# The feed-forward block's up projection takes x times the norm's weights; the norm's root multiplies the projections in their banks

## The reference, cut to what matters

```python
def rms_norm_2(x, g):
    xf = x.astype(jnp.float32)
    y = xf * lax.rsqrt(jnp.mean(xf * xf, axis=-1, keepdims=True) + EPS)
    return (y * g.astype(jnp.float32)).astype(x.dtype)

def conv_ffn_2(h, w_up, conv_w, conv_b, w_down):
    a = h @ w_up
    a = lax.conv_general_dilated(a, conv_w[:, None, :], ...) + conv_b   # 3 taps along the tokens, each channel by itself
    g, u = jnp.split(a, 2, axis=-1)
    return (jax.nn.gelu(g, approximate=True) * u) @ w_down

for l in range(DEPTH_2):
    ...
    x = x + rms_norm_2(memory_cross_attention(h, mem_n, ...), mem_post_g[l])
    h = rms_norm_2(x, ffn_pre_g[l])
    x = x + rms_norm_2(conv_ffn_2(h, ffn_w_up[l], ffn_conv_w[l], ffn_conv_b[l], ffn_w_down[l]), ffn_post_g[l])
```

## Time and profile before

| | |
|---|---|
| device time, median of 3 runs | 3171.85 us (3171.47 to 3172.96) |
| device time of the profiled execution | 3170.39 us |
| its span in the trace | 3168.6 us |
| busy of the span: PE, DVE, ACT, POOL | 2932.6 us (93%), 1545.3 (49%), 1279.6 (40%), 329.7 (10%) |
| mean clock granted to PE | 0.962 of full speed |

### The profile page before, as it was taken

One profiled execution on the slowest core, in us unless ns is written; L12 is line 12 of the kernel. 1 busy time (PEld: TensorE's weight loads), 2 busy tenths in 40 slices (PEclk: granted clock), 3 DMA queues, 4 the chain that ended last, 5 costly groups with the idle time before them and its releaser, 6 DMA issues. The chain is left out here.

```text
span 3168.6 us, 38772 instructions
## 1 busy us (share of the span) xinstructions
PE 2932.6 (93%) x14576; PEld 2294.1 (72%) x14576; DVE 1545.3 (49%) x2161; ACT 1279.6 (40%) x1866; POOL 329.7 (10%) x286
## 2 busy tenths in 40 slices
PE   6989887999989999899899889999899999899997
PEld 2879765688768888576577668886675677578885
DVE  3357246565545443356663454443465663454433
ACT  3751424532243332534563343333425652433333
POOL 0010004500001100004000111100004001011100
PEclk8999999999999999999799999999999899999999
DMA  5100210045412222120032122222120131122222
GB/s 234 67 28 1 87 53 1 7 167 169 149 68 105 93 93 93 62 80 14 27 120 80 53 80 93 93 104 78 68 80 1 45 129 54 53 93 94 105 102 80
DMA packets 43552, 254.04 MB, mean 80 GB/s; under 512 B 4608, under 2 KB 6784, under 8 KB 15872
## 3 DMA queue, kind: packets, MB, share of 16 engines
q1 hardware_dynamic: 43392, 251.87, 22.3%
HBM read 249.75 MB, written 2.10 MB: 79 GB/s over the span
## 5 line engine op out<-in xcount | busy, mean ns | idle before, releaser
L238 DVE TENSOR_TENSOR ring_lo<-ring,ring_hi 128x2048 fp32r<-128x2048 f32 x201 | 460.8, 2293 | 807.5 <-ACT ring_hi L231 807.5
L231 ACT ACTIVATE ring_hi<-ring 128x2048 fp32r<-128x2048 f32 x201 | 383.8, 1909 | 456.0 <-PE bank L289 341.0
L289 PE MATMUL bank<-h_hi,ring_hi 128*128 128x512 f32 x1360 | 546.5, 402 | 17.1 <-DVE mix_lo L1605 6.4
L289 PE MATMUL bank<-h_hi,ring_lo 128*128 128x512 f32 x1360 | 534.3, 393 | 0.0
L1417 PE MATMUL bank<-h_hi,ring_hi 128*128 128x512 f32 x960 | 374.2, 390 | 5.7 <-DVE ring_lo L238 5.7
L1421 PE MATMUL bank<-h_hi,ring_lo 128*128 128x512 f32 x960 | 373.5, 389 | 0.0
L1420 PE MATMUL bank<-h_lo,ring_hi 128*128 128x512 f32 x960 | 373.5, 389 | 0.0
L289 PEld LDWEIGHTS bank<-h_hi,ring_hi 128*128 128x128 f32 x1360 | 257.2, 189 | 80.9 <-issue 15.6
L289 PEld LDWEIGHTS bank<-h_hi,ring_lo 128*128 128x128 f32 x1360 | 257.1, 189 | 60.0
L289 PE MATMUL bank<-h_lo,ring_hi 128*128 128x512 f32 x624 | 243.9, 391 | 0.0
L1417 PEld LDWEIGHTS bank<-h_hi,ring_hi 128*128 128x128 f32 x960 | 180.2, 188 | 45.4 <-issue 5.5
(11 more groups left out here) (453 smaller groups left out, 5018.2 us busy)
## 6 DMA issues: line engine op xcount, KB each, us to landing
ring<-in_stream SPq DMA_DIRECT2D x209, 1024.0 KB, 4.8
mod_w<-in_stream SPq DMA_DIRECT2D x64, 256.0 KB, 5.1
xT<-in_xT SPq DMA_DIRECT2D x2, 2048.0 KB, 14.8
const<-in_const SPq DMA_DIRECT2D x1, 2306.5 KB, 15.8
par<-in_par SPq DMA_DIRECT2D x3, 696.0 KB, 4.0
memT<-in_memT SPq DMA_DIRECT2D x2, 1024.0 KB, 4.8
out<-xT SPq DMA_DIRECT2D x1, 2048.0 KB, 6.3
ctxT<-in_ctxT SPq DMA_DIRECT2D x1, 1024.0 KB, 4.8
```

Source lines behind the costliest of these rows:

```text
L231: nc.scalar.activation(self.slab_hi(slab + j), self.slab(slab + j), ACT.Copy).then_inc(slab_rounded, 1)
L238: nc.vector.tensor_tensor(lower, self.slab(slab + j), self.slab_hi(slab + j).bitcast(F32), ALU.subtract)\
L289: ins = nc.tensor.matmul(out, lhsT, rhs, start=start and w is w_hi and x is x_hi, stop=stop and w is w_lo)
```

## The change

The next norm's squares, their sums and the second root leave `project`, and with them the scaling of `xT` into `hT`. The stage ends behind the first root. A new class `Unnormed` takes the place of `Norms` in the second block's `ffn`: DVE scales the projected tiles and adds them to `xT`, ACT writes `h_hi` from `xT` times the gain, DVE writes `h_lo` with the gain in the same instruction, ACT squares `xT`, and DVE adds up the squares. PE sums them over the channels in one matmul behind the first two pairs, and then ACT takes the root. In `taps` DVE multiplies both banks of each pair by the root; only then may ACT's `centers` read them. In `project`, ACT also copies banks 1 to 3 into `raw`, so that PE may write these banks early.

```diff
+        class Unnormed:
+            def banks_left(self, pe):
+                pe.wait_ge(self.post.scale_ready.sem, self.post.scale_ready.at(1))
+                pe.wait_ge(self.post.left.sem, self.post.left.at(len(self.post.LEFT)))
+            def sum(self, pe):
+                pe.wait_ge(self.squares_added.sem, self.squares_added.at(KT - 1))
+                nc.tensor.matmul(bank[:, 6, :], con("ones"), self.square_place(0), start=True, stop=True).then_inc(self.summed.sem, 1)
+            def scalar(self, act):
...
+                    nc.scalar.activation(split_hi(n), xT[:, n, :], ACT.Identity, scale=self.gain(n)).then_inc(self.upper_ready.sem, 1)
+                    if n == 1:
+                        self.halfway_scalar(act)
+                    if n >= SQUARES:
+                        act.wait_ge(self.squares_added.sem, self.squares_added.at(n - SQUARES + 1))
+                    nc.scalar.activation(self.square_place(n), xT[:, n, :], ACT.Square).then_inc(self.squared.sem, 1)
+                act.wait_ge(self.summed.sem, self.summed.at(1))
+                root_of_mean(act, self.scale, bank[:, 6, :]).then_inc(self.scale_ready.sem, 1)
+            def vector(self, dve):
+                post, LAG = self.post, 2
+                dve.wait_ge(post.scale_ready.sem, post.scale_ready.at(1))
+                dve.wait_ge(post.left.sem, post.left.at(len(post.LEFT)))
+                for n in range(KT + LAG):
+                    if n < KT:
+                        src = post.raw[:, n, :] if n == 0 or n in post.LEFT else bank[:, n, :]
+                        nc.vector.scalar_tensor_tensor(post.raw[:, n, :], src, post.gain(n), post.scale, ALU.mult, ALU.mult)\
+                            .then_inc(post.normed.sem, 1)
+                        if n not in post.pool_tiles:
+                            dve.wait_ge(post.normed.sem, post.normed.at(n + 1))
+                            nc.vector.tensor_tensor(xT[:, n, :], xT[:, n, :], post.raw[:, n, :], ALU.add)\
+                                .then_inc(post.added_by_dve.sem, 1)
+                    if n >= LAG:
+                        k = n - LAG
+                        dve.wait_ge(self.upper_ready.sem, self.upper_ready.at(k + 1))
+                        nc.vector.scalar_tensor_tensor(split_lo(k), xT[:, k, :], self.gain(k), split_hi(k).bitcast(F32),
+                                                       ALU.mult, ALU.subtract).then_inc(self.lower_ready.sem, 1)
+                    if n == 3:
+                        self.halfway_vector(dve)
+                    if n >= 5:
+                        self.add_square(dve, n - 4)
+                for n in range(KT + LAG - 4, KT):
+                    self.add_square(dve, n)
...
@@ ffn, tensor: two_pairs and what follows
+                        for k in range(AHEAD):
+                            for n in range(2):
+                                first = part_of(n, k)
...
+                        for k in range(AHEAD):
+                            for n in range(2, 4):
+                                part_of(n, k)
...
                 two_pairs()
+                if norm.late:
+                    norm.sum(pe)
@@ ffn, scalar
                 def centers(n, j):
-                    act.wait_ge(pair_done.sem, pair_done.at(n + 1))
+                    done = norm.scaled if norm.late else pair_done
+                    act.wait_ge(done.sem, done.at(n + 1))
@@ ffn, vector
                 def taps(n, j):
+                    out_ap = pair(j)
+                    if norm.late:
+                        dve.wait_ge(pair_done.sem, pair_done.at(n + 1))
+                        for s in range(2):
+                            last = nc.vector.tensor_tensor(out_ap[s], out_ap[s], norm.scale, ALU.mult)
+                        last.then_inc(norm.scaled.sem, 1)
                     dve.wait_ge(center_ready.sem, center_ready.at(n + 1))
@@ project
                     post.square(act, n)
+                    if n in post.LEFT:
+                        nc.scalar.activation(post.raw[:, n, :], bank[:, n, :], ACT.Copy).then_inc(post.left.sem, 1)
                 post.rms(act)
-                ws.round_second(act, (at + KT * KT) // SLAB + 1)
-                post.next_squares(act)
-                post.next_rms(act)
```

More of the change, by code:

```diff
@@ L699, in build_program @@
             halfway_scalar = halfway_vector = between_scalar = between_vector = None
+            late = False
             def gpsimd(self, pool):
@@ L719, in build_program, with __init__ @@
         class PostNorm:
-            def __init__(self, gain, raw, squares, scales, by_pool=True):
+            LEFT = (1, 2, 3)
+            def __init__(self, gain, raw, squares, scales, by_pool=True, followed=True):
                 if not by_pool:
@@ L1424, in two_pairs @@
                 def two_pairs():
-                    ws.first_two(pe, first_slab)
-                    pe.wait_ge(banks_free.sem, banks_free.at(2))
+                    if not norm.late:
+                        ws.first_two(pe, first_slab)
+                        pe.wait_ge(banks_free.sem, banks_free.at(2))
                     def part_of(n, k):
@@ L1438, in part_of @@
                         return first
-                    for k in range(TOGETHER):
+                    if norm.late:
+                        assert first_slab == ws.begun and not ws.pending
+                        norm.banks_left(pe)
+                        pe.wait_ge(slab_split, ws.count(first_slab) - WHOLE_SLABS)
+                        for k in range(AHEAD):
+                            for n in range(2):
+                                first = part_of(n, k)
+                                if k == 0 and n == 0:
+                                    first.then_inc(slab_begun, 1)
+                        pe.wait_ge(slab_split, ws.count(first_slab + 1) - WHOLE_SLABS)
+                        for k in range(AHEAD):
+                            for n in range(2, 4):
+                                part_of(n, k)
+                        ws.begun += 2
+                    for k in range(AHEAD if norm.late else 0, TOGETHER):
                         for n in range(4):
@@ L1448, in two_pairs @@
                                 first.then_inc(slab_begun, 1)
-                norm.sums(pe, range(1))
+                if not norm.late:
+                    norm.sums(pe, range(1))
                 two_pairs()
+                if norm.late:
+                    norm.sum(pe)
                 for j in range(2, rest):
+                    if norm.late and j == 3:
+                        pe.wait_ge(norm.scale_ready.sem, norm.scale_ready.at(1))
                     products(j, j)
@@ L1505, in vector @@
             def vector(dve):
-                nc.vector.memset(small[:, 255:256], 0.0).then_inc(banks_free.sem, per_turn)
+                if not norm.late:
+                    nc.vector.memset(small[:, 255:256], 0.0).then_inc(banks_free.sem, per_turn)
                 def lower(k):
@@ L1532, in vector @@
                 norm.vector(dve)
+                if norm.late:
+                    nc.vector.memset(small[:, 255:256], 0.0).then_inc(banks_free.sem, per_turn)
+                    dve.wait_ge(norm.scale_ready.sem, norm.scale_ready.at(1))
                 loop(dve, taps, ws.halve, first_lowers)
@@ L3026, in post @@
             def post(gain):
-                return PostNorm(lambda n: p2(gain, 1, n), raw, squares2, scales2)
+                return PostNorm(lambda n: p2(gain, 1, n), raw, squares2, scales2, followed=False)
             class Memory:
```

53 lines of the change are left out of this document (40 added, 13 removed).

## The result

The changed kernel took 3180.9 us (median of 6 runs, 3175.42 to 3185.73), the kernel before 3171.66 us beside it (6 runs, 3165.83 to 3172.96): a ratio of 1.0037, with a 95% interval of 1.0024 to 1.0051 (the quotient of the two medians, 1.0029, lies in it). The forecast was 3186 us, with 3175 to 3193. All that follows reads the profiled execution of 3182.45 us (span 3180.6), against the one of before of 3170.39 us (span 3168.6).

A forecast was written before the change was run, and what follows sets the result against it. PE, busy 93% of the span, was taken as the bound. Each layer's terms sum to 7.3 us, 14.7 in all; on the profiled 3170.39 that is 3185.1, and with the median 1.5 above, 3186 us (range 3175 to 3193).

The forecast's parts named there:

- The handover's gain: Between the first root and the up projection: PE begins the up projection at 1825.1 us, 12.2 us earlier than before.
- The second wait: In the handover, after PE's first 12 matmuls (4.2 us): PE waits again, some 2 us near 1829, going on at 1831.4.
- the 0.8 us that I had put at half price: In the handover: the 2.0 us of idle time could lower PE's clock, costing 1.5 us; half taken, 0.8.
- Pair 2: Up projection, behind the late second root: begins at 1858.8 us, 2.5 us earlier than before, after PE waits some 7 us.
- Pair 3: Up projection: its slab waits for pairs 0 and 1; begins at 1874.8 us, 1.0 us later, PE idle 3.5 us.
- pair 4: Up projection, behind pair 3's wait: 2.5 us late, with 1.5 us counted for PE's lower clock.
- The multiplications: DVE's two multiplications in each pair's banks: 1.28 us a pair, bounds 1.1 and 1.5.
- The loop: Pairs in `Fori`: slab 0.36 us late, paid about every second pair, 0.16 us a pair, 2.2 us for 14 pairs.
- The entry of `Fori`: Where `Fori` begins: the slab's halving has 0.27 us left before PE needs it, so 0.95 us are lost.
- the down projection: At the down projection's slab: 0.42 us left before PE needs it, so 0.9 us are lost.
- The sum: Each layer 2.5 (fourth pair, with clock) + 0.8 + 0.95 + 2.2 + 0.9 = 7.3 us, 14.7 us in all.
- A sign that misled: Up projection: the forecast is wrong if pair 3 begins before 1873.8 us.

The follow-up runs named there:

- after_again: The changed kernel unaltered, run once more on the chip of three other follow-up kernels, against the kernel before at 3166.05 us: 3180.79 us (5 runs), ratio 1.0047.

## Why the prediction held, step by step

**The handover's gain** was right: PE begins 5.68 us behind the root's end (forecast 5.7, before 17.95). That it fits so closely is in part luck. DVE begins 0.49 us behind the root's end and not 0.37, and needs 5.14 us up to the first lower half and not 5.25.

**The second wait** was forecast at 2.0 us and is 0.69. I had counted 4.2 us for the first 12 matmuls; they took 5.2, since the first ten of them ran at the lower clock. The third operand tile was there 0.4 us sooner than counted (+11.56 us, counted +12.0). The windows of the changed kernel (columns as above) show the lower clock, and no second fall behind the wait:

```profile
1823.30:1829.20 5.90, 5.21 (x13) 3.82 (x13) 5.87 (x7) 3.94 (x7) 3.93 (x1) 0.60 0.50 178
1829.20:1848.00 18.80, 18.80 (x83) 15.58 (x84) 12.31 (x18) 6.26 (x9) 1.78 (x2) 1.00 0.11 37
1856.30:1870.30 14.00, 13.89 (x48) 10.95 (x48) 8.15 (x13) 7.24 (x8) 2.60 (x2) 0.79 0.21 77
1872.50:1886.00 13.50, 13.48 (x53) 11.03 (x54) 6.95 (x9) 3.88 (x4) 1.29 (x1) 0.88 0.22 78
```

A mean clock of 0.60 in the first and 1.00 in the second: the 0.8 us that I had put at half price did not occur, and the second root came 0.66 us sooner than counted (34.46 us behind the first, forecast 35.12).

**Pair 2** begins at +38.72 us (forecast +39.42), 3.2 us earlier than before instead of 2.5. The wait of some 7 us is 6.96.

**Pair 3** begins at +54.90 us, 0.44 later than before (forecast 1.0). The chain of pairs 0 and 1 took 16.27 us, from 1856.12 to the halving's end at 1872.39 (counted 15.95). PE waited 2.29 us, not 3.5, since it began pair 2 at the lower clock (13 matmuls, 0.79 in the third window) and ended it late: the pair took 13.9 us. The prediction has 12.5 us for it (1858.8 to 1871.3), 1.6 more than PE's 10.88, and doesn't say what the 1.6 are. This is the same loss in another place: what I counted as idle PE spent as slow matmuls. Behind pair 3 the clock is 0.88 over 13.5 us, 1.5 us lost as forecast, and pair 4 is 1.9 us late (forecast 2.5).

**The multiplications** were priced at 1.28 a pair and take 1.29 to 1.30. The view of their line:

```profile
L1629 DVE TENSOR_TENSOR bank<-bank,scales x88: 689/691/700, 1856.1 to 3029.0; 128x512 f32<-128x512 f32 x88
```

That is 691 ns each, 0.60 us from one to the next. By the Trainium skill, page "VectorE: DVE Perf Modes", section on the TRN2 errata, my estimate was 1.32 for both. The trace's 1.29 to 1.30 lies between the sum's 1.28 and that.

**The loop is the term of the sum that was mis-sized**: 0.16 us a pair and 2.2 us for 14 pairs forecast; from the first wait in `Fori` to the next is 22.35 us (1941.33 to 1963.68) where two pairs of before take 2 x 10.88, so it is 0.295 us a pair and 4.1 us in all. (Half of the forecast's own 0.36 us is 0.18 a pair and 2.5 us, not 0.16 and 2.2.) The pattern, a wait for `ring_lo` at every second pair, is as forecast. One pair of the chain on DVE's timeline and then on ACT's, of the changed kernel, shows what I had undercounted:

```profile
1952.53 1.30 DVE L1629 TENSOR_TENSOR bank<-bank,scales 128x512 f32<-128x512 f32 x2 [0.46 <-PE bank L1504]
...
1961.23 2.29 DVE L238 TENSOR_TENSOR ring_lo<-ring,ring_hi 128x2048 fp32r<-128x2048 f32 x1 [2.53 <-ACT ring_hi L231]
```

```profile
1954.11 1.45 ACT L1586 ACTIVATE mix<-bank,par 128x512 f32<-128x512 f32 x2 [4.38 <-DVE bank L1629]
...
1958.73 0.63 ACT L1591 ACTIVATE mix<-mix 128x512 f32<-128x512 f32 x1 [3.17 <-DVE mix L1636]
1959.28 1.92 ACT L231 ACTIVATE ring_hi<-ring 128x2048 fp32r<-128x2048 f32 x1
```

PE's timeline has the start of the pair that runs beside them, and the matmuls ahead of and behind the wait of 1963.68:

```profile
1952.33 0.40 PE L1500 MATMUL bank<-h_hi,ring_hi 128*128 128x512 f32 x1
...
1963.02 0.39 PE L1504 MATMUL bank<-h_hi,ring_lo 128*128 128x512 f32 x1
...
1964.01 0.40 PE L1503 MATMUL bank<-h_lo,ring_hi 128*128 128x512 f32 x1
```

From the pair's start at 1952.33, DVE scales at +0.20, ACT's `centers` follow at +1.78 (0.28 us behind the scaling's end), and the halving ends at +11.19 (counted 1.73 and 11.10). With 0.14 us to start, the slab is 0.45 us late, not 0.36. And a stall costs more than its lateness: the first matmul behind it is followed by the next only after 0.33 us where 0.23 is the rule. That makes some 0.55 of the 0.59 us by which two pairs are longer. The idle time shown, 0.28 us, says only half of it, since matmuls of 0.39 us overlap when nothing stops them: starts at 1963.02, 1963.68 and 1964.01 are 0.53 us more apart than two steps of 0.23.

**The entry of `Fori` and the down projection.** The idle times are 0.92 us (forecast 0.95) and 0.38 (forecast 0.9). Counted as above, from start to start of the matmuls, the two stalls cost 1.2 and 0.65 us. The forecast's 0.95 does not follow from its own figures: 1.31 us more work with 0.27 us left is 1.04.

**The sum.** Pair 4 late by 1.9, no second loss in the handover, 1.2 at the entry, 4.1 in the loop and 0.65 at the down projection are 7.9 us of the measured 8.15. The forecast's 7.3 came near by luck in part: the loop was 1.9 us and the entry 0.25 us too low, and against them the handover's second wait was 0.8 us, pair 4 0.6 us and the down projection 0.25 us too high.

**The median** came out 5 us below the forecast though the stretch was longer. The profiled execution of the changed kernel is 4.3 us shorter outside the two stretches than the one of before on which the sum stands. Some 1.6 us of this are seen ahead of the first stretch, where PE waits 3.19 us in both kernels. In the kernel before, eight matmuls behind this wait ran slow (the row at 1768.49 in the earlier trace rows); in this execution none did, as PE's timeline and the windows of the changed kernel and of the kernel before show:

```profile
1768.29 0.49 PE L289 MATMUL bank<-h_hi,ring_hi 128*128 128x512 f32 x1 [3.19 <-DVE mix_lo L1719]
```

```profile
1768.20:1772.20 4.00, 3.91 (x17) 3.22 (x18) 4.00 (x7) 4.00 (x7) 0.00 (x0) 1.00 0.54 184
```

```profile
1768.40:1772.40 4.00, 3.91 (x10) 3.10 (x11) 4.00 (x7) 4.00 (x7) 0.00 (x0) 0.57 0.48 156
```

The changed kernel's second profiled execution (after_again) has 0.57 again at this place, so it belongs to the execution and not to the change. Why the rest was shorter is not settled; the kernel before itself ranged from 3158.5 to 3172.8 us over its 25 runs. In the second comparison the medians lie 14.7 us apart, the very sum that was forecast.

**A sign that misled.** The prediction calls itself wrong if pair 3 begins before 1873.8 us, and pair 3 begins at 1872.52. But the root's end, from which the layer is counted, came at 1817.62 instead of 1819.38 in this execution. Counted from the root, pair 3 is 0.44 us later than before, and the forecast's sign doesn't apply. Such a sign has to be put as a distance, not as a time.

## What to carry to other kernels

Work moved off the start of a stage is paid in the stage: before moving a factor behind the product, add up the chain that makes the next weights, across all engines with its handoffs, and compare it with PE's time for one step. Half-idle engines say nothing about slack, since they may be idle waiting for one another. If the chain is too long, reorder it before trimming it: here one round that was moved into ACT's idle time bought back 9 us a layer, and together with two slabs made ahead it turned a loss of 0.4% into a gain of 0.7%.

## What the hardware did that I had not expected

- DVE held POOL up for longer than POOL held DVE: of the changed kernel's first two additions on DVE, the one beside POOL took 1.63 us (at 1819.56) and the other 0.69 (at 1821.89). An addition of 128x512 took POOL 1.27 us at its shortest, on POOL's timeline of the kernel before:

```profile
1820.25 1.27 POOL L823 TENSOR_TENSOR xT<-xT,raw 128x512 f32<-128x512 f32 x1 [57.41 <-DVE raw L809]
```

  It took 3.93 us beside DVE's halving, while the halving took 2.29 us as elsewhere, on POOL's and DVE's timelines of the changed kernel:

```profile
1823.98 3.93 POOL L825 TENSOR_TENSOR xT<-xT,raw 128x512 f32<-128x512 f32 x1 [3.34 <-DVE raw L888]
```

```profile
1824.48 2.29 DVE L238 TENSOR_TENSOR ring_lo<-ring,ring_hi 128x2048 fp32r<-128x2048 f32 x1
```

- After 6.96 us of idle time 13 matmuls ran at the lower clock of 1.2 GHz, at once. After 2.29 us seven did, and after the waits of 0.92 us or less in `Fori` none: from 1918.97 to 2075.43 us the granted clock is 1.00.
- The same idle time in the same place does not always bring the lower clock. Of the ten profiled executions that I have of all kernels, nine have about eight slow matmuls behind the wait of 3.2 us near 1768 us in the first layer, and one, that of the changed kernel shown above, has none. Behind the waits at pairs 2 and 3 it came in both profiled executions of the changed kernel. For a stretch as short as these a forecast of the loss (1.5 us here) is a chance and not a fixed price.
